# Column sums of six norms taken where x is made, the square root's table loaded ahead, and splits of weights moved behind the root, in a sixteen-layer float32 kernel

## What is computed

```python
def rms_norm(x, g):
    xf = x.astype(F32)
    y = xf * lax.rsqrt(jnp.mean(xf * xf, axis=-1, keepdims=True) + EPS)
    return (y * g.astype(F32)).astype(x.dtype)

for i in range(DEPTH):
    hn = rms_norm(h, norm_mix[i])
    ...
    hn = rms_norm(h, norm_ffn[i])
    h = h + hier_moe(hn, router_group_w[i], ...)
```

## Time and profile before

| What | Value |
|---|---|
| three runs of the kernel | 2534.71, 2528.01 and 2537.45 us; median 2534.71 |
| the profiled execution | 2531.46 us, its span 2529.7 us |
| busy, share of the span | PE 88%, weight loads 71%, DVE 45%, ACT 35%, POOL 2% |
| mean granted TensorE clock | 0.928 of full speed |
| HBM read | 672.17 MB, 266 GB/s over the span |
| norms | 11 reciprocals of 1752 ns (L554), 11 roots (L548), 8 table loads of 1283 ns in front of a root |

### The profile page before, as it was taken

The page is one execution under the profiler, slowest core; times in us unless marked ns, Lnnn a source line. Parts: engine busy times, 40 slices in busy tenths (PEclk is TensorE's granted clock), DMA queues, the critical chain, the costliest instruction groups (busy, mean ns, idle before and its releaser), DMA issues. The chain is left out here.

```text
span 2529.7 us, 45042 instructions
## 1 busy us (share of the span) xinstructions
PE 2218.7 (88%) x19490; PEld 1793.3 (71%) x19490; DVE 1136.5 (45%) x2008; ACT 884.1 (35%) x1470; POOL 58.3 (2%) x78
## 2 busy tenths in 40 slices
PE   6998788887885999869999998787898998898998
PEld 6967466654553996757777776554778997777997
DVE  5355345223422643543333323424746555746554
ACT  4443332233211442322222222333444444544442
POOL 0000000000000000000000000000000000000000
PEclk8999898999998999989999999787988999988999
DMA  6594998999999557559999999797413555413551
GB/s 237 167 321 173 357 380 343 397 402 404 403 400 371 183 184 266 216 211 378 414 414 416 412 413 367 307 358 273 145 34 122 183 173 166 138 46 123 183 174 38
DMA packets 254367, 676.26 MB, mean 267 GB/s; under 512 B 12624, under 2 KB 65872, under 8 KB 254160
## 3 DMA queue, kind: packets, MB, share of 16 engines
q1 hardware_dynamic: 238832, 614.77, 64.4%
q0 software_dynamic: 15328, 58.50, 6.0%
HBM read 672.17 MB, written 1.05 MB: 266 GB/s over the span
## 5 line engine op out<-in xcount | busy, mean ns | idle before, releaser
L444 PE MATMUL bank<-xx,high 128*128 128x256 f32 (+1 forms) x3296 | 636.3, 294 | 38.3 <-DVE xx L583 25.8
L444 PEld LDWEIGHTS bank<-xx,high 128*128 128x128 f32 (+1 forms) x3296 | 526.4, 195 | 95.4 <-issue 69.5
L444 PE MATMUL bank<-xx,low 128*128 128x256 f32 (+1 forms) x1648 | 476.2, 289 | 0.0
L444 PEld LDWEIGHTS bank<-xx,low 128*128 128x128 f32 (+1 forms) x1648 | 322.2, 196 | 1.6
L393 DVE TENSOR_TENSOR low<-lane,high 128x1024 fp32r<-128x1024 f32 (+1 forms) x112 | 130.7, 1170 | 346.6 <-ACT high L382 346.6
L382 ACT ACTIVATE high<-lane 128x1024 fp32r<-128x1024 f32 (+1 forms) x112 | 113.0, 1012 | 322.8 <-PE bank L444 322.8
L444 PE MATMUL bank<-hx,high 128*128 128x256 f32 x1056 | 199.6, 290 | 0.0
L444 PEld LDWEIGHTS bank<-hx,high 128*128 128x128 f32 x1056 | 165.8, 192 | 17.7 <-issue 15.1
L444 PE MATMUL bank<-hx,low 128*128 128x256 f32 x528 | 149.8, 284 | 0.0
L1335 ACT ACTIVATE hs<-bank 64x256 f32<-64x256 f32 x64 | 24.2, 378 | 297.8 <-PE bank L1322 297.8
L1342 DVE TENSOR_TENSOR hs<-hs,bank 64x256 f32<-64x256 f32 x64 | 27.1, 423 | 212.7 <-ACT hs L1335 212.7
(11 more groups left out here) (547 smaller groups left out, 4086.9 us busy)
## 6 DMA issues: line engine op xcount, KB each, us to landing
ring__13<-in_expert_w_gu SPq DMA_DIRECT2D x52, 1024.0 KB, 10.4
ring__12<-in_expert_w_gu SPq DMA_DIRECT2D x51, 1024.0 KB, 10.9
ring__14<-in_expert_w_gu SPq DMA_DIRECT2D x51, 1024.0 KB, 10.5
ring__56<-in_expert_w_gu SPq DMA_DIRECT2D x26, 1024.0 KB, 11.2
ring__12<-in_expert_w_down SPq DMA_DIRECT2D x26, 1024.0 KB, 8.6
ring__154<-in_expert_w_gu SPq DMA_DIRECT2D x26, 1024.0 KB, 11.1
ring__55<-in_expert_w_gu SPq DMA_DIRECT2D x25, 1024.0 KB, 10.8
ring__14<-in_expert_w_down SPq DMA_DIRECT2D x25, 1024.0 KB, 9.7
```

The source lines that it names most:

```text
L444: done = pe.matmul(out, a.bitcast(F32R), b.bitcast(F32R), start=it["start"] and k == 0 and q == 0 and not halves, stop=stop)
```

## The change

Five things change together.

1. `Early` now takes all eight chunks. The next stage's `squares` and `sums` do nothing where a norm has an early part, and the sum's last matmul raises `colsum`. Chunks 4 to 7 come after the end of the last projection on ACT and PE, on the same two scratch tiles.
2. `ended` gives, beside x, the whole sum (`csum`) in place of the sum of chunk 3.
3. `set_table` applies a function to one element, so that its table is loaded at that place: Sqrt ahead of the last projection of every stage that makes x, ahead of the root in fox, ret and mix0, and ahead of the squares of the heads in the mixers; Exp in the expert layers behind the root.
4. ACT takes the root first and splits weights behind it (ret, mixers, feed-forward); in the expert layers the root comes ahead of the gained copies of x.
5. DVE's first splits of weights, which stood ahead of the reciprocal, come between the chunks of x.

```diff
+        zeros, spare = space(ctx, "zeros", 1), space(ctx, "spare", 1)
...
             def squares(self, e, which):
                 s = sq_v if which else sq_a
-                for c in range(self.early, KC):
-                    if c % 2 != which:
-                        continue
+                if self.early:
+                    return
+                for c in range(which, KC, 2):
...
             def sums(self, pe):
-                if not self.early:
-                    self.bk.next(self.name)
+                if self.early:
+                    self.bk.release(self.name)
+                    return
+                self.bk.next(self.name)
...
-            def split_dve(self, dve, halfway=None, part=None):
+            def split_dve(self, dve, between=None, part=None):
                 first, end = part or (0, len(self.pieces))
                 for i in range(first, end + 2):
-                    if halfway and i == len(self.pieces) // 2:
-                        halfway()
+                    if between and i in between:
+                        between[i]()
...
                 pe.wait_ge(*early_a.at((self.name, c)))
-                pe.matmul(banks[self.name][:, 0:self.n], ones, self.scratch[c % 2], start=c == 0, stop=False).then_inc(
-                    *early_p.up((self.name, c)))
+                s, k = (csum, self.name) if c == KC - 1 else (early_p, (self.name, c))
+                pe.matmul(banks[self.name][:, 0:self.n], ones, self.scratch[c % 2], start=c == 0, stop=c == KC - 1).then_inc(*s.up(k))
+
+        def set_table(act, f):
+
+            act.activation(spare, eps, f)
...
-            for c in range(max(0, len(g.items) - n0 - 2), 4):
+            for c in range(min(4, max(0, len(g.items) - n0 - 2)), KC):
                 early.pe(pe, c)
...
         def out_proj_act(act, g, early):
             n0 = g.last[0, 0]
+            set_table(act, ACT.Sqrt)
             for it in g.act(act):
                 c = it["at"] - n0 - 1
                 if 0 <= c < 4:
                     early.act(act, c)
+            for c in range(4, KC):
+                early.act(act, c)
...
             def act(act):
                 events_wait(act, opened)
-                norm.squares(act, 0)
+                norm.root(act)
                 for c in range(0, KC, 2):
                     act.activation(xt[:, c, :], x[:, c, :], ACT.Copy, scale=gm[:, c:c + 1]).then_inc(*xg_a.up(K(c)))
-                norm.root(act)
+                set_table(act, ACT.Exp)
...
                 norm.squares(act, 0)
+                set_table(act, ACT.Sqrt)
+                norm.root(act)
                 proj.act_high(act, 2)
-                norm.root(act)
                 norm.split_act(act)
...
                 norm.squares(dve, 1)
-                proj.dve_low(dve, 2)
                 norm.rstd(dve)
-                norm.split_dve(dve)
+                norm.split_dve(dve, {2: lambda: proj.dve_low(dve, 1), 4: lambda: proj.dve_low(dve, 2)})
...
-                if v:
-                    proj.dve_low(dve, 3)
                 yield
...
-                    norm.split_dve(dve, lambda: proj.dve_low(dve, 4))
+                    norm.split_dve(dve, {2: lambda: proj.dve_low(dve, 2), 4: lambda: proj.dve_low(dve, 3), 8: lambda: proj.dve_low(dve, 4)})
...
-                if v:
-                    up.dve_low(dve, 1)
                 yield
...
-                    norm.split_dve(dve, lambda: up.dve_low(dve, 2))
+                    norm.split_dve(dve, {2: lambda: up.dve_low(dve, 1), 5: lambda: up.dve_low(dve, 2)})
...
         def ended(x_done, early_name):
-            return x_done(7) + [(early_p, (early_name, 3))]
+            return x_done(7) + [(csum, early_name)]
```

More of the change, by code:

```diff
@@ L164, in build @@
         eid = space(ctx, "eid", 2 * NX + 2, dt=I32, rows=1)
-        zeros = space(ctx, "zeros", 1)
+        zeros, spare = space(ctx, "zeros", 1), space(ctx, "spare", 1)
         base_slots = [space(ctx, f"ring{i}_", SLOT) for i in range(3)]
@@ L512, in build, with __init__ @@
         class Norm:
-            def __init__(self, name, xs, n, sq, rs, ready, early=0, bk=banks):
+            def __init__(self, name, xs, n, sq, rs, ready, early=False, bk=banks):
                 self.bk = bk
@@ L531, in order @@
             def order(self):
-                return range(self.early, KC) if self.early else [*range(0, KC, 2), *range(1, KC, 2)]
+                return [*range(0, KC, 2), *range(1, KC, 2)]
             def sums(self, pe):
-                if not self.early:
-                    self.bk.next(self.name)
-                    for s, k in self.bk.freed(self.name):
-                        pe.wait_ge(*s.at(k))
+                if self.early:
+                    self.bk.release(self.name)
+                    return
+                self.bk.next(self.name)
+                for s, k in self.bk.freed(self.name):
+                    pe.wait_ge(*s.at(k))
                 for c in self.order():
@@ L542, in sums @@
                 i.then_inc(*csum.up(self.name))
-                if self.early:
-                    self.bk.release(self.name)
             def root(self, act):
@@ L1155, in moe @@
             iota = V("iota")
-            norm = Norm(early_name, x, T, tmp, rs, x_ready, early=4)
+            norm = Norm(early_name, x, T, tmp, rs, x_ready, early=True)
             gm = V("norm_ffn", 8 * L, 8)
@@ L1730, in dve @@
                 events_wait(dve, opened)
-                norm.squares(dve, 1)
                 for c in range(1, KC, 2):
@@ L2077, in mixer @@
             else:
-                norm = Norm(early_in or name, xs, T, yt, rs, x_ready or (lambda c: []), early=4 if early_in else 0, bk=bk)
+                norm = Norm(early_in or name, xs, T, yt, rs, x_ready or (lambda c: []), early=bool(early_in), bk=bk)
                 norm.split_to(tm, xh, xl, gains(L, 0, 0, v))
@@ L2358, in act @@
                 events_wait(act, opened)
+                norm.squares(act, 0)
+                yield
+                if v and not L:
+                    set_table(act, ACT.Sqrt)
+                norm.root(act)
+                if v:
+                    proj.act_high(act, 4)
                 act.activation(nw.rearrange("p a c t -> p (a c) t").bitcast(F32R), bc(V("mask_z"), [P, 4, P], 1), ACT.Copy).then_inc(
                     *gate_a.up(K("zero")))
-                norm.squares(act, 0)
-                if v:
-                    proj.act_high(act, 4)
-                yield
-                norm.root(act)
                 if v:
@@ L2800, in ffn @@
             hh, hl = hx[:, :, 0, :], hx[:, :, 1, :]
-            norm = Norm(early_in or name, xs, T, sq, rs, x_ready, early=4 if early_in else 0, bk=bk)
+            norm = Norm(early_in or name, xs, T, sq, rs, x_ready, early=bool(early_in), bk=bk)
             norm.split_to(tm, xh, xl, gains(L, 1, 24, v))
@@ L2867, in act @@
                 norm.squares(act, 0)
-                if v:
-                    up.act_high(act, 2)
                 yield
@@ L2872, in act @@
                 if v:
+                    up.act_high(act, 2)
                     norm.split_act(act)
```

## The result

The changed kernel took 2574.68 us (median of 4 runs, 2566.45 to 2582.79) against 2535.77 before: a ratio of 1.0159, 95% interval 1.0121 to 1.0198. I had forecast 2537 us, and 0.09 for a slowdown. It came out 26 us above the top of my range. The profiled execution is the one of 2566.45 us, span 2564.7.

The account below looks back on a forecast made before the run. Most stages were taken as bound by a full DMA or PE, so a late first product ends its stage late. Seam terms summed to +4.4 us; set on the four-run mean of 2532.9, that gave 2537 us, range 2526 to 2549.

Parts of the forecast that it names:

- price p: Weight loads into moved slots: extra share of each packet's time, read from `tab` as 0 to 2%, taken as nothing.
- rival 3: Ring slots 32 bytes beyond a multiple of 256 make weight packets dearer: 1% adds 11 us, 2548 us; chance 0.10.
- turning point 0.8%: Weight packets: the extra cost that turns the answer to slower, adding 8.6 us to the forecast's 4.4.
- number of slices: Whole kernel: 17 slices of 63.2 us with DMA at nine tenths or more, 1075 us, would grow with packet cost.
- moe0 +2.4: First expert layer: `wr` asked for 2.36 us later, behind the whole sum, so logits and everything behind move along.
- moe1 +1.8: Second expert layer: `wr` asked for at 1088.35 instead of 1086.57, delaying the logits; ends 0 and +2.5 us.
- ret -0.8: ret: root 1.96 us sooner, less one low part of 1.18 behind the reciprocal, so 0.8 us gained.
- mix0 +1.0: First mixer: sums 0.6 us sooner, but low parts of 0.4 and 1.18 behind the reciprocals; 1.0 us lost.
- ffn0 and ffn1 +1.0 each: Feed-forward stages: root 0.2 us sooner, but a low part of 1.18 behind the reciprocal; 1.0 us lost each.
- mix1 -1.2: Second mixer: root 3.0 us sooner, less moved work of 0.4, 1.18 and 0.2, so 1.2 us gained.
- final -0.75: Last norm: root at 2514.5 instead of 2515.28, with reciprocal, scaling and output following; 0.75 us gained.
- nine places: Whole kernel: the change works at eight stage seams that move, and fox, where the root's order stays.

Follow-up runs that it names:

- aligned: The changed kernel plus 56 columns of padding behind the one-column spare tile, slots again on multiples of 256 bytes: 2537.7 us, 1.0014 of the kernel before.
- shift_all: The kernel before plus one unused column behind the zeros tile, everything behind it 32 bytes beyond a multiple of 256: 2565.9 us, 1.0119 of the kernel before.

## Why the prediction was wrong

**The step that failed** is the price p of a weight packet in a moved slot. The sum had it at nothing, and rival 3, which named it, bounded it too low; with it falls that rival's 0.10. Place and mechanism were named: slots 32 beyond a multiple of 256, weight packets dearer, turning point 0.8%. I wrote "so p is 0 to 2%"; in the full stretch it is 5.6%, 2.7% on the ring's queue and 16% on the lanes'. I had read p from `tab`, 72 packets of 6 KB, in a stretch as full as moe1's (18.9% beside the ring's 82.2%), and called it the same thing. It was on the lanes' queue and at a place off the boundary, and there it doesn't pay: its median is 234 ns, which is also what the undisturbed packets of 1, 2 and 4 KB (46, 84 and 159 ns) give for 6 KB, an estimate. But `tab` does pay a little elsewhere. In the kernels that moved it by a further 32, 64 and 128 bytes its median is 238, 236 and 238 ns and its mean 243 instead of 237; the lanes' 4 KB packets pay 19% already at 32 beyond. I had also let the lanes' queue go by: it carries a fifth of the bytes of a full stretch of moe1. A bound that a single other transfer gives isn't a bound for this one, and the range should have reached to a price of some per cent on what keeps the DMA engines full.

The number of slices in that estimate was too high: 17 full ones at 5.6% would be 60 us, and the loss is 39 against the kernel before and 30 for the place alone. moe1's full part of some 440 us (seven slices) times 5.6% is 25; it got 20.8 longer. fox shows no loss beyond its spread.

**The terms of the order**, read from `aligned`, against the kernel before:
- moe0 +2.4: the logits start 6.54 us behind the last update instead of 4.11, +2.4. Right; the stage's length doesn't resolve it (578.1 and 582.2 us with the old order, 583.6 to 587.8 in three profiles with the new and `wr` asked for late).
- moe1 +1.8: 8.47 instead of 6.24, +2.2 (`wr` took 0.1 us longer to land). Right at the front, but not at the end: the stage took 653.9, 654.0 and 654.4 us with the new order and 654.6 and 654.3 with the old. The late start isn't swallowed: a place that I had left out gives it back (below).
- ret -0.8: the root comes 3.65 behind the last update instead of 5.63, 2.0 sooner as worked out, but with the new order the stage took between 273.0 and 277.9 us in six kernels. Not resolved.
- mix0 +1.0: -0.1. The stage takes 185 to 189 us with either order. Not resolved.
- ffn0 and ffn1 +1.0 each: +0.7 and +0.9. In size right, but not by my working: squares 4 and 6 stand 1.26 apart instead of 1.15, the reciprocal comes 0.1 us later and not 0.2 sooner (4.08 against 3.99 in both), and PE's long run starts 2.0 us later (12.24 against 10.22 behind the update), twice my figure. The clock came back at 15.8 and 15.6 us against 15.7 and 15.2. That 2.0 late leave only 0.7 and 0.9 at the end is not explained; part of the agreement is luck.
- mix1 -1.2: +2.3. The root came 2.8 sooner and DVE's last chunk of x 1.3 sooner, as forecast. But the last low part, put between the last chunks, made PE stop for 0.71 us, and the clock came back 2.7 us later than before. This is the one stage that clearly went the wrong way.
- final -0.75: -0.7.

**A tenth place.** I had counted nine places at which the change works. Inside moe1, between expert products, the second context mixer takes its norm, and there `nw` and the squares changed places on ACT as in mix0. The context's last update, 478 us into the stage, is still 2.6 us late in `aligned`. The root behind it, before and in `aligned`:

```profile
1570.70 0.47 ACT L548 ACTIVATE rs<-bank,vec 128x256 f32<-128x256 f32 x1 [3.34 <-PE bank L541]
...
1577.71 0.47 ACT L548 ACTIVATE rs<-bank,vec 128x256 f32<-128x256 f32 x1 [1.65 <-PE bank L543]
```

It stands 7.01 us behind that update before (which starts at 1563.69) and 4.79 in `aligned` (1572.92), 2.2 sooner. The reciprocal behind it stands at 7.6 in every profile of the old order and at 5.4 in every one of the new. This gives back about 2.2 us and cancels moe1's +1.8.

The measured sum of all places is the ratio of `aligned`, 1.0014 or +3.6 us (-1 to +8), against my +4.4. The order of work is thus as small as forecast, though in part by errors that cancel (mix1 came out 3.5 us worse than its term, mix0 1.1 better, and the tenth place 2.2 better), and nearly all of the loss is the tile that came with it.

The Trainium skill (DMA: Bandwidth & Descriptors, How a descriptor splits into AXI transactions) says that a descriptor which does not start on a 256-byte boundary has its first transaction start at the boundary below, and that the bytes fetched for nothing cost beats too. On the boundary the runs agree: 256 bytes are free, 32, 64 and 128 are not. The page words it for reads, and here it is the side written to, SBUF, that moved. By its rule a 4 KB packet takes 129 beats instead of 128 at 32 beyond and 132 at 128 beyond; worked out from that, an estimate, the price would be 0.8 and 3%. The runs show about one price for all three places, seven times the first of these.

## What to carry to other kernels

Before a tile is added ahead of buffers that large transfers fill, print the addresses: here 32 bytes of scratch cost 1.2%, and padding to a multiple of 256 gave it back. To test for it, put an unused tile into the unchanged kernel; a price read from one other transfer, with another packet size and at another place, is not a bound. At a seam, count a break in PE's first products not by its length but by when the granted clock returns, and read that in windows of both kernels; small loads that wait for a stage to open belong ahead of it.

## What the chip showed that I had not expected

- A 4 KB packet of the lanes' queue takes 159 ns (median of 14016) with slots on a multiple of 256 and 189 at 32 beyond, 188 at 64, 186 at 128; one of the ring's queue 159 and in the same order 162, 162, 160 (of 99200; means 163.5 and 166.5, 167.2, 166.6). Packets of 1 and 2 KB keep their medians of 46 and 84 ns.
- It isn't the traffic of the other queue: in `shift_all`, the lane packets that begin in a microsecond in which the ring's queue uses under 0.05 of the engines have a median of 192 ns (1800 of them), in the kernel before 159.
- Why the queue that GpSimd feeds pays 16% and SyncE's 2.7%, and why `tab`, on the former and at 32 beyond, paid nothing, stays open. So does what in the engines or the memory makes a moved packet dearer. Lane loads on another engine's queue were not tried.
- A stop of 0.71 us within PE's first products kept its clock at 1.2 GHz until 19.2 us behind the last update of x, against 13.6 and 15.2 in two profiles without it, and cost mix1 4.9 and 2.9 us.
